# Value products of two attentions taken by head pairs, and low halves of the second attention's outputs made on GpSimd

## Chip, cores and metric

One core of one Trainium2 chip. The metric is the device time of one execution in microseconds (us): before the change 1065.82 us, median of 3 runs (1065.64 to 1067.22). The engines are named as in the profile: PE is TensorE (PEld its weight loads), DVE is VectorE, ACT is ScalarE, POOL is GpSimd, and SP issues most transfers.

## The reference, cut to what matters

Two transformer blocks run one after the other on 256 tokens of width 1024: the first has two layers, the second one (`DEPTH_2 = 1`), so the kernel has layers 0 to 2. Layer 0 has an attention with 8 heads (query and key width 96, value width 64), layer 1 is convolutional, and layer 2 has an attention with 16 heads of width 64. In both attentions the keys are 256 tokens and 256 context tokens:

```python
s = jnp.einsum('bqhd,bhkd->bhqk', qi, kt).astype(jnp.float32) * scale   # first attention
p = jax.nn.softmax(s, axis=-1).astype(vt.dtype)
return jnp.einsum('bhqk,bhkd->bqhd', p, vt)
# second attention: a bias and a mask are added to the scores of the 256 token keys,
# softmax runs over token and context keys together, then p @ v as above
```

After each attention comes an output projection (1024 by 1024), an update of x, a norm and a feed-forward layer. All is fp32.

## The kernel before, in words

**Projections.** Large products are split in high and low halves: weights arrive in a ring of six raw slots (`w_raw`, 512 KB each), ACT casts the high half (`w_hi`, L703), DVE subtracts to get the low half (`w_lo`, L1205), and PE does three products (L1902 to L1904). Activations are held as `h_hi` and `h_lo`. SP issues the loads in the order of a fixed table (`ada_issue_table`, L98): weight w waits for the split of weight w-6, and `at[w]` says how many of the conditioning blocks (`ada`, through four slots of `a_raw`) are issued ahead of weight w. DVE sums one such block per instruction (L1245); a slot is loaded again only when its block has been summed.

**Attention.** The unit is a block n: one head, one tile of 128 queries, 512 keys. Pass j of the loop handles blocks 2j and 2j+1, which are the two heads of a pair at query tile j % 2; so a head pair p takes passes 2p and 2p+1, that is blocks 4p to 4p+3. PE runs, in pass j: the transposes of blocks 2j and 2j+1 (`turn`, L2069, four of 128 by 128 each), the scores of pass j+2 (`scores`, L2060, two products of 512 columns), and the value products of pass j-1 (`weigh`, L2083: eight products with 64 stationary and 128 moving columns, four key tiles by two heads; the two heads write the two halves of the output partitions). After the second `weigh` of a pair four more products (L2091) spread the inverted row sums beside the output in the same bank. Every fp32 product that isn't a transpose leaves two records.

On the other engines pass j has: DVE finds the row maxima of pass j+1 (first attention L1342 and L1344; second attention adds bias and mask in place, L1332, and reduces, L1339); ACT takes the exponentials of pass j (L810) and copies the transposed blocks of pass j-1 from PSUM to `probT` (L822); in the second attention DVE does every fourth of these copies (L1354). For an output, ACT copies it (L829), DVE multiplies it by the inverted sums (L1364), ACT makes its high half (L833) and DVE its low half (`out_lo`, L1368), which the output projection waits for (`o_lo`). In the first attention DVE also sums one conditioning block a pass; in passes 1 to 4 both split one weight.

Score blocks use four banks, transposed blocks two (block n waits until block n-2 is copied out), outputs two. `probT` has two homes of one pass each: a copy of pass j waits for `weigh(j-2)`, by the semaphore `pv_done`, which rises by two each time.

**Around it.** After the first attention ACT issues the load of the second context (`big<-ctx`, 1 MB, L1062), squares its eight tiles when it has landed (L749), and POOL adds these squares and then those of x (`add_squares`, L636); PE takes the sums (L1986) within the last block of the output projection. After the second attention the output projection has eight weights, of which the fourth is split in pass 4 already and the fifth at the projection's start.

Of the kernel before, what the change touches and what calls it, by code (L numbers as in the profile page):

```python
# [9 lines left out]
P = 128  # L10
# [87 lines left out]
def ada_issue_table():  # L98

    at = {RING + n: 17 + n for n in range(4)}  # L100
    at.update({14: 21, 17: 23, 18: 25, 19: 28, 20: 30, 21: 37, 22: 38, 23: 39, 24: 40, 25: 44, 35: 48})
# [100 lines left out]
def program(nc, weights, ada, xt_in, ctx1_in, ctx2_in, params_in, consts_in, rpb_in, out_t):  # L202
# [5 lines left out]
    with ctx:  # L208
# [39 lines left out]
        probT = work[:, PROBS * 512:].rearrange("p (b e k t) -> p b e k t", b=2, e=2, k=4)  # L248
# [318 lines left out]
        def _(sp):  # L567
            def load_w(w, s):

                if w - RING in WHOLE:  # L570
                    sp.wait_ge(w_used, w - RING + 1)
                elif w >= RING:
                    sp.wait_ge(split_done, splits_to(w - RING))
# [45 lines left out]
        def _(pool):  # L619
# [69 lines left out]
            for h in range(BIAS_HOMES, NA_H):  # L689
                mask_bias(h)  # L690
            add_squares(7)

        @block.scalar
        def _(act):
# [118 lines left out]
            def attention(name, heads, at0, o0, query_scale, w_next, begun=0):  # L813

                def turned(n):
                    if name == "na" and n % 4 == 3:
                        return
                    b = wait_tile(act, (name, "tr", n))
                    j, e = n // 2, n % 2
                    if j >= 2:  # L820
                        act.wait_ge(pv_done, at0 + 2 * (j - 1))
                    nc.scalar.copy(probT[:, j % 2, e, :, :], b[:, :].rearrange("p (k q) -> p k q", k=4))\  # L822
# [369 lines left out]
        def _(dve):  # L1192
# [154 lines left out]
            def attention(name, heads, at0, o0, w_next):  # L1347

                def turned(n):
                    b = wait_tile(dve, (name, "tr", n))  # L1350
                    j, e = n // 2, n % 2
                    if j >= 2:
                        dve.wait_ge(pv_done, at0 + 2 * (j - 1))
                    nc.vector.tensor_copy(probT[:, j % 2, e, :, :], b[:, :].rearrange("p (k q) -> p k q", k=4))\  # L1354
# [19 lines left out]
                for j in range(heads):  # L1374
# [11 lines left out]
                    if j >= 4 and j % 2 == 0:  # L1386
# [5 lines left out]
                out_lo(heads // 2 - 2)  # L1392
# [506 lines left out]
        def _(pe):  # L1899
# [163 lines left out]
            def attention(name, heads, at0, rows, values, values_ready, begun):  # L2063
# [574 lines left out]
```

## Time and profile before

| | us |
|---|---|
| median of 3 runs | 1065.82 |
| the profiled execution | 1069.91 |
| its span | 1068.1 |
| PE busy | 1048.2 (98%) |
| DVE busy | 779.7 (73%) |
| ACT busy | 552.6 (52%) |
| POOL busy | 115.7 (11%) |
| chain that ended last | PE 88%, DVE 5%, DMA 3%, issue 2% |

The span is the profiled execution's, which is 4.1 us slower than the median of the timed runs, 1.8 us of this outside the span. PE's ends are modelled, so its busy time is not PE at its peak; what a stage costs is read from the starts of its groups.

### The profile page before, as it was taken

The numbers are of one execution on the slowest core, as the hardware profiler recorded it, in microseconds if no ns is written. First come the engines' busy times: TensorE is split into PE (matmuls) and PEld (weight loads), VectorE is DVE, ScalarE is ACT, GpSimd is POOL, SyncE is SP. The second block draws the span as 40 slices with busy tenths as digits, with TensorE's granted clock in tenths as the row PEclk, the third lists the DMA queues.
The fourth block names the chain that finished last, engine by engine and source line by source line (L and its number), as shares of the span: only waits on it lengthen the run. The fifth ranks groups of instructions, "written<-read, shape, count | busy, mean of one in ns | idle before, by whom it ended". The sixth has DMA issues, their size and how long they took to land.

```text
span 1068.1 us, 20130 instructions
## 1 busy us (share of the span) xinstructions
PE 1048.2 (98%) x7862; PEld 950.1 (89%) x7862; DVE 779.7 (73%) x1381; ACT 552.6 (52%) x951; POOL 115.7 (11%) x133
## 2 busy tenths in 40 slices
PE   6999999999999999999999999999999999999998
PEld 1887787999999989888999999888866799999998
DVE  2697777788887678847677775697439877777876
ACT  4646766444344485555445444546337665454442
POOL 2200012000000037410000000400331020000000
PEclk9999998999999999999999999999999999999999
DMA  9982274989898726465787775387550054656551
GB/s 361 410 315 93 76 246 181 345 344 337 330 354 319 272 64 253 138 255 204 274 288 273 280 269 207 111 291 261 135 99 31 4 187 146 197 166 206 166 189 41
DMA packets 68593, 232.83 MB, mean 218 GB/s; under 512 B 12144, under 2 KB 12432, under 8 KB 68144
## 3 DMA queue, kind: packets, MB, share of 16 engines
q1 hardware_dynamic: 62496, 227.20, 59.6%
q0 software_dynamic: 5888, 3.73, 1.6%
q10 hardware_dynamic: 144, 1.05, 0.3%
q8 instruction: 39, 0.64, 0.2%
q14 instruction: 26, 0.21, 0.1%
HBM read 230.85 MB, written 1.05 MB: 217 GB/s over the span
## 4 chain that ended last, share of the span: by engine, by line
PE 88%; DVE 5%; DMA 3%; issue 2%; ACT 1%; SPq 0%; DVEq 0%; ACTq 0%
PE bank L1902 26%; PE bank L1904 25%; PE bank L1903 25%; PE bank L2427 3%; PE bank L1929 2%; DMA w_raw<-weights 2%; DMA a_raw<-ada 2%; PE bank L2060 2%; DVE bank L1332 1%; PE bank L2069 1%; PE bank L2083 1%; PE bank L1986 1%; DVE w_lo L1205 1%; PE bank L1958 1%; PE bank L2309 1%
## 5 line engine op out<-in xcount | busy, mean ns | idle before, releaser
L1902 PE MATMUL bank<-h_hi,w_hi 128*128 128x256 f32 (+2 forms) x1408 | 404.8, 288 | 3.4 <-DVE h_lo L1853 1.7
L1904 PE MATMUL bank<-h_hi,w_lo 128*128 128x256 f32 (+2 forms) x1408 | 401.7, 285 | 0.0
L1903 PE MATMUL bank<-h_lo,w_hi 128*128 128x256 f32 (+2 forms) x1408 | 401.1, 285 | 0.0
L1205 DVE TENSOR_TENSOR w_lo<-w_raw,w_hi 128x1024 fp32r<-128x1024 f32 x271 | 327.6, 1232 | 64.8 <-ACT w_hi L703 63.4
L703 ACT CAST w_hi<-w_raw 128x1024 fp32r<-128x1024 f32 x271 | 275.5, 1045 | 65.2 <-PE bank L1904 56.8
L1902 PEld LDWEIGHTS bank<-h_hi,w_hi 128*128 128x128 f32 x1408 | 267.5, 190 | 11.4 <-issue 5.2
L1903 PEld LDWEIGHTS bank<-h_lo,w_hi 128*128 128x128 f32 x1408 | 268.0, 190 | 1.3 <-issue 0.2
L1904 PEld LDWEIGHTS bank<-h_hi,w_lo 128*128 128x128 f32 x1408 | 268.0, 190 | 1.0
L1902 PE MATMUL bank<-g_hi,w_hi 128*128 128x256 f32 x528 | 148.9, 282 | 0.0
L1904 PE MATMUL bank<-g_hi,w_lo 128*128 128x256 f32 x528 | 148.8, 282 | 0.0
L1903 PE MATMUL bank<-g_lo,w_hi 128*128 128x256 f32 x528 | 148.7, 282 | 0.0
L636 POOL TENSOR_TENSOR big<-big 128x256 f32<-128x256 f32 x39 | 40.5, 1039 | 595.9 <-ACT big L749 594.2
L1902 PEld LDWEIGHTS bank<-g_hi,w_hi 128*128 128x128 f32 x528 | 99.5, 188 | 0.3 <-issue 0.2
L1245 DVE SCALAR_TENSOR_TENSOR a_raw<-a_raw,bias 128x1024 f32<-128x1024 f32 x80 | 98.8, 1239 | 1.1 <-DMA a_raw<-ada 1.0
L1904 PEld LDWEIGHTS bank<-g_hi,w_lo 128*128 128x128 f32 x528 | 99.5, 189 | 0.0
L1903 PEld LDWEIGHTS bank<-g_lo,w_hi 128*128 128x128 f32 x528 | 99.5, 188 | 0.0
L868 ACT ACTIVATE work<-bank 128x256 f32<-128x256 f32 x44 | 16.9, 384 | 133.3 <-PE bank L1904 133.3
L1902 PE MATMUL bank<-w_hi,h_hi 128*128 128x512 f32 (+1 forms) x180 | 72.1, 400 | 1.7 <-ACT big L1015 1.7
L1903 PE MATMUL bank<-w_lo,h_hi 128*128 128x512 f32 (+1 forms) x180 | 70.8, 393 | 0.0
L1904 PE MATMUL bank<-w_hi,h_lo 128*128 128x512 f32 (+1 forms) x180 | 70.7, 393 | 0.0
L1473 DVE TENSOR_TENSOR work<-work,bank 128x256 f32<-128x256 f32 x44 | 18.5, 421 | 57.4 <-ACT work L868 57.4
L761 ACT ACTIVATE h_hi<-big,mods 128x256 fp32r<-128x256 f32 x56 | 26.6, 505 | 42.1 <-DVE big L1293 41.9
(210 smaller groups left out, 1241.0 us busy)
## 6 DMA issues: line engine op xcount, KB each, us to landing
w_raw<-weights SPq DMA_DIRECT2D x281, 512.0 KB, 4.9
a_raw<-ada SPq DMA_DIRECT2D x140, 512.0 KB, 5.4
vals<-ada SPq DMA_DIRECT2D x4, 512.0 KB, 8.7
a_raw<-rpb POOLq DMA_DIRECT2D x9, 224.0 KB, 14.7
bias<-rpb POOLq DMA_DIRECT2D x7, 224.0 KB, 8.2
xT<-xt SPq DMA_DIRECT2D x1, 1024.0 KB, 9.5
big<-ctx SPq DMA_DIRECT2D x1, 1024.0 KB, 14.3
big<-ctx ACTq DMA_DIRECT2D x1, 1024.0 KB, 8.0
```

Of the source, the lines that this page charges most:

```text
L636: nc.gpsimd.tensor_tensor(v[:, 0, :], v[:, 0, :], v[:, k, :], ADD).then_inc(added, 1)
L703: nc.scalar.copy(w_hi[:, s, :], w_raw[:, s, :]).then_inc(hi_done, 1)
L761: nc.scalar.activation(h_hi[:, k, c0:c0 + T], tmp[:, k, :], ACT.Identity, bias=sh).then_inc(hhi_ready, 1)
L1205: nc.vector.tensor_tensor(w_lo[:, s, :], w_raw[:, s, :], w_hi[:, s, :].bitcast(fp), SUB)\
L1245: nc.vector.scalar_tensor_tensor(out=a_raw[:, s, :], in0=a_raw[:, s, :], scalar=1.0, in1=cond_row[later], op0=MUL, op1=MUL, accum_out=flat ...
L1473: nc.vector.tensor_tensor(gate_f[:, s, :], act_f[:, s, :], bank[b][:, T:2 * T], MUL).then_inc(ff_mul, 1)
L1902: nc.tensor.matmul(out, a_hi, b_hi, start=start, stop=False)
L1903: nc.tensor.matmul(out, a_hi, b_lo, start=False, stop=False)
L1904: return nc.tensor.matmul(out, a_lo, b_hi, start=False, stop=stop)
L1929: ins = nc.tensor.matmul(b[32 * part:32 * part + 2, :], cs[:, g // (MODS // AGRP), k, :], home[:, s, (k % 2) * 512:(k % 2 + 1) * 512], sta ...
L2060: nc.tensor.matmul(b[:, :], q[:, t * P:(t + 1) * P], k, start=True, stop=True)\
L2427: ins = nc.tensor.matmul(b[:, 0:T], w_raw[:, w % RING, k * P:(k + 1) * P], h_whole[k], start=(k == 0), stop=(k == KT - 1))
```

## The change

Value products now run once per head pair: `weigh(p)` follows pass 2p+2 and takes eight products with 256 moving columns (both query tiles, read from `probT` in two stretches of 128) where two calls had eight of 128 each. It waits for all four blocks of the pair. `probT` gets a second home for a whole pair in two raw weight slots, those of weights `W_OUT0 + 4` and `W_OUT2 + 4` and the ones after them. So SP waits at each of these two weights until the attention's last value product is done, and ACT waits, before the first copy into that home, for the splits of the last weights that lay there; and conditioning blocks up to the 40th are issued ahead of weight 19 (`W_OUT0 + 4`) instead of between weights 19 and 24. `pv_done` now rises by two per pair. In the second attention the low halves of outputs 0 to 6 are made on POOL; DVE makes the last one.

```diff
-    at.update({14: 21, 17: 23, 18: 25, 19: 28, 20: 30, 21: 37, 22: 38, 23: 39, 24: 40, 25: 44, 35: 48})
+    at.update({14: 21, 17: 23, 18: 25, 19: 40, 25: 44, 35: 48})
...
-        probT = work[:, PROBS * 512:].rearrange("p (b e k t) -> p b e k t", b=2, e=2, k=4)
+        by_pair = lambda a: a.rearrange("p (t e k q) -> p t e k q", t=2, e=2, k=4)
+        spare = (W_OUT0 + LEAD) % RING
+        probT = [by_pair(work[:, PROBS * 512:]), by_pair(w_raw[:, spare:spare + 2, :].rearrange("p s b -> p (s b)"))]
...
+                if w == W_OUT0 + LEAD:
+                    sp.wait_ge(pv_done, MLA_H)
+                if w == W_OUT2 + LEAD:
+                    sp.wait_ge(pv_done, MLA_H + NA_H)
...
+            for p in range(NA_H // 2 - 1):
+                pool.wait_ge(o_hi, 16 + p + 1)
+                nc.gpsimd.tensor_tensor(h_lo[:, p, 0:T], o_unit[:, p % 2, :], h_hi[:, p, 0:T].bitcast(fp), SUB)\
+                    .then_inc(o_lo, 1)
...
+                    if n == 4:
+                        act.wait_ge(split_done, splits_to(w_next - 1))
                     b = wait_tile(act, (name, "tr", n))
                     j, e = n // 2, n % 2
-                    if j >= 2:
-                        act.wait_ge(pv_done, at0 + 2 * (j - 1))
+                    if j >= 4:
+                        act.wait_ge(pv_done, at0 // 2 + 2 * (j // 2 - 1))
...
+                    if name == "na":
+                        dve.wait_ge(o_lo, o0 + p)
...
-                    if j >= 4 and j % 2 == 0:
+                    if name == "mla" and j >= 4 and j % 2 == 0:
                         out_lo(j // 2 - 2)
...
-                out_lo(heads // 2 - 2)
+                if name == "mla":
+                    out_lo(heads // 2 - 2)
...
-                def weigh(j):
-                    p, t = j // 2, j % 2
-                    if j == 0:
+                def weigh(p):
+                    if p == 0:
                         pe.wait_ge(v_ready, values_ready)
-                    pe.wait_ge(*turned_by(name, at0, 2 * j))
-                    pe.wait_ge(*turned_by(name, at0, 2 * j + 1))
-                    b = write_tile(pe, (name, "o", p)) if t == 0 else bank[tiles[(name, "o", p)][0]]
+                    for n in range(4 * p, 4 * p + 4):
+                        pe.wait_ge(*turned_by(name, at0, n))
+                    b = write_tile(pe, (name, "o", p))
                     for kt in range(4):
                         for e in range(2):
-                            ins = nc.tensor.matmul(b[e * VH:(e + 1) * VH, t * P:(t + 1) * P], values(2 * p + e, kt),
-                                                   probT[:, j % 2, e, kt, :], start=(kt == 0), stop=(kt == 3))
+                            out = b[e * VH:(e + 1) * VH, 0:T].rearrange("p (t q) -> p t q", t=2)
+                            ins = nc.tensor.matmul(out, values(2 * p + e, kt), probT[p % 2][:, :, e, kt, :],
+                                                   start=(kt == 0), stop=(kt == 3))
...
-                    if j:
-                        weigh(j - 1)
-                weigh(heads - 1)
+                    if j and j % 2 == 0:
+                        weigh(j // 2 - 1)
+                weigh(heads // 2 - 1)
```

## Rows read from the trace of the kernel before

**Rows 1.** Windows: stretch, then busy us per engine, PE clock, DMA share, GB/s.

```profile
117.00:145.50 28.50, 28.46 (x251) 19.50 (x249) 25.02 (x56) 25.07 (x55) 0.00 (x0) 1.00 0.57 194
796.00:849.50 53.50, 52.49 (x506) 35.02 (x505) 45.85 (x87) 40.28 (x101) 3.59 (x4) 1.00 0.07 21
```

**Rows 2.** Timeline of PE, second attention: start us, us, engine, line, operation.

```profile
800.85 1.09 PE L2083 MATMUL bank<-work,vals 128*64 128x128 f32 x16
...
835.17 1.09 PE L2083 MATMUL bank<-work,vals 128*64 128x128 f32 x16
836.19 1.09 PE L2069 MATMUL bank<-con,work 128*128 128x128 f32 x8
837.21 1.13 PE L2060 MATMUL bank<-big 64*128 64x512 f32 x4
838.27 1.09 PE L2083 MATMUL bank<-work,vals 128*64 128x128 f32 x16
839.20 0.61 PE L2091 MATMUL bank<-con,rinv 128*64 128x128 f32 x8
839.73 1.09 PE L2069 MATMUL bank<-con,work 128*128 128x128 f32 x8
...
846.50 0.66 PE L2069 MATMUL bank<-con,work 128*128 128x128 f32 x4 [0.52 <-ACT work L822]
847.09 2.04 PE L2083 MATMUL bank<-work,vals 128*64 128x128 f32 x32
```

**Rows 3.** Timeline of PE, first attention.

```profile
118.18 1.88 PE L2060 MATMUL bank<-big 96*128 96x512 f32 x4
119.90 1.04 PE L2069 MATMUL bank<-con,work 128*128 128x128 f32 x8
120.78 1.88 PE L2060 MATMUL bank<-big 96*128 96x512 f32 x4
122.59 1.09 PE L2083 MATMUL bank<-work,vals 128*64 128x128 f32 x16
...
143.06 1.98 PE L2083 MATMUL bank<-work,vals 128*64 128x128 f32 x32
144.86 0.62 PE L2091 MATMUL bank<-con,rinv 128*64 128x128 f32 x8
```

**Rows 4.** Timeline of ACT, first attention: copies out of the transposed banks.

```profile
122.87 0.61 ACT L822 COPY work<-bank 128x512 f32<-128x512 f32 x1
...
138.70 0.59 ACT L822 COPY work<-bank 128x512 f32<-128x512 f32 x1
...
142.73 1.07 ACT L822 COPY work<-bank 128x512 f32<-128x512 f32 x2
```

**Rows 5.** Timeline of ACT, second attention: exponentials of blocks 5 and 13.

```profile
801.33 0.69 ACT L810 ACTIVATE work<-bank,nmax 128x512 f32<-128x512 f32 x1
...
815.19 0.69 ACT L810 ACTIVATE work<-bank,nmax 128x512 f32<-128x512 f32 x1
```

**Rows 6.** Timeline of DVE, second attention.

```profile
818.75 0.42 DVE L1368 TENSOR_TENSOR h_lo<-ada_s,h_hi 128x256 fp32r<-128x256 f32 x1
819.08 0.62 DVE L1332 TENSOR_TENSOR bank<-bank,a_raw 128x256 f32<-128x256 f32 x1
...
847.20 0.69 DVE L1354 COPY work<-bank 128x512 f32<-128x512 f32 x1
```

**Rows 7.** DMA issues from 140 to 175: KB each, median us to landing.

```profile
w_raw<-weights SPq DMA_DIRECT2D x9, 512.0 KB, 5.5
...
big<-ctx ACTq DMA_DIRECT2D x1, 1024.0 KB, 8.0
```

**Rows 8.** Timeline behind the first attention: ACT, POOL and PE's weight loads.

```profile
154.48 2.57 ACT L749 ACTIVATE big<-big 128x256 f32<-128x256 f32 x8 [5.55 <-DMA big<-ctx]
...
155.28 13.26 POOL L636 TENSOR_TENSOR big<-big 128x256 f32<-128x256 f32 x10 [83.18 <-ACT big L749]
...
168.66 1.41 PEld L1986 LDWEIGHTS bank<-con,big 128*128 128x128 f32 x12 [0.16 <-issue]
```

More of the change, by code:

```diff
@@ L246, in program @@
         prob = work[:, 0:PROBS * 512].rearrange("p (b t) -> p b t", b=PROBS)
-        probT = work[:, PROBS * 512:].rearrange("p (b e k t) -> p b e k t", b=2, e=2, k=4)
+        by_pair = lambda a: a.rearrange("p (t e k q) -> p t e k q", t=2, e=2, k=4)
+        spare = (W_OUT0 + LEAD) % RING
+        probT = [by_pair(work[:, PROBS * 512:]), by_pair(w_raw[:, spare:spare + 2, :].rearrange("p s b -> p (s b)"))]
+        assert spare == (W_OUT2 + LEAD) % RING and spare + 1 < RING
         nmax = sb("nmax", [P, 32])
@@ L817, in turned @@
                         return
+                    if n == 4:
+                        act.wait_ge(split_done, splits_to(w_next - 1))
                     b = wait_tile(act, (name, "tr", n))
                     j, e = n // 2, n % 2
-                    if j >= 2:
-                        act.wait_ge(pv_done, at0 + 2 * (j - 1))
-                    nc.scalar.copy(probT[:, j % 2, e, :, :], b[:, :].rearrange("p (k q) -> p k q", k=4))\
+                    if j >= 4:
+                        act.wait_ge(pv_done, at0 // 2 + 2 * (j // 2 - 1))
+                    nc.scalar.copy(probT[j // 2 % 2][:, j % 2, e, :, :], b[:, :].rearrange("p (k q) -> p k q", k=4))\
                         .then_inc(pT_ready, 1)
@@ L1351, in turned @@
                     j, e = n // 2, n % 2
-                    if j >= 2:
-                        dve.wait_ge(pv_done, at0 + 2 * (j - 1))
-                    nc.vector.tensor_copy(probT[:, j % 2, e, :, :], b[:, :].rearrange("p (k q) -> p k q", k=4))\
+                    if j >= 4:
+                        dve.wait_ge(pv_done, at0 // 2 + 2 * (j // 2 - 1))
+                    nc.vector.tensor_copy(probT[j // 2 % 2][:, j % 2, e, :, :], b[:, :].rearrange("p (k q) -> p k q", k=4))\
                         .then_inc(pT_other, 1)
@@ L2085, in weigh @@
                             if kt == 3:
                                 ins.then_inc(pv_done, 1)
-                    if t == 1:
-                        pe.wait_ge(rinv_ready, at0 // 4 + p + 1)
-                        for n in range(4):
-                            e, t = n % 2, n // 2
-                            ins = nc.tensor.matmul(b[e * VH:(e + 1) * VH, T + t * P:T + (t + 1) * P],
-                                                   rinv[:, 4 * p + n:4 * p + n + 1].broadcast_to([P, VH]), ident,
-                                                   start=True, stop=True)
-                        ins.then_inc(full_of((name, "o", p)), 1)
+                    pe.wait_ge(rinv_ready, at0 // 4 + p + 1)
@@ L2096, in attention @@
+                    for n in range(4):
+                        e, t = n % 2, n // 2
+                        ins = nc.tensor.matmul(b[e * VH:(e + 1) * VH, T + t * P:T + (t + 1) * P],
+                                               rinv[:, 4 * p + n:4 * p + n + 1].broadcast_to([P, VH]), ident,
+                                               start=True, stop=True)
+                    ins.then_inc(full_of((name, "o", p)), 1)
                 for j in range(begun, 2):
```

## The prediction

> **What bounds the kernel now.** I read the windows by stage first. In both attentions PE is busy nearly throughout: 28.46 of 28.50 us in the first, 52.49 of 53.50 us in the second [rows 1]. But DVE has 25.02 of 28.50 and 45.85 of 53.50 us of its own there, and ACT is close behind it. So PE sets the end with little to spare, and work taken from PE shortens a stage only until a maximum, an exponential or a copy is what PE waits for. The starts of PE's groups give dense prices. Second attention [rows 2]: a pass's transposes 1.02 us (836.19 to 837.21), scores 1.06 (to 838.27), a value call that a transpose follows 1.02 (835.17 to 836.19), one that the inverse sums follow 0.93 (838.27 to 839.20), the inverse sums 0.53. A head pair therefore takes 2 x (1.02 + 1.06) + 1.02 + 0.93 + 0.53 = 6.64 us. DVE in its turn needs about 6.6 us a pair: 5.73 busy (45.85 / 8) and the gaps between dependent instructions. First attention [rows 3]: scores 1.72 us ahead of a transpose (118.18 to 119.90), 1.81 ahead of a value call (120.78 to 122.59), transposes 0.93; a pair 2 x (0.93 + 1.81) + 1.02 + 0.93 + 0.53 = 7.96 us.
>
> **The value products.** No row has 64 stationary by 256 moving columns. Two calls back to back, 16 products of 128 columns, take 1.80 us (143.06 to 144.86) [rows 3]. The two heads use the two halves of PE's columns and overlap. This shows against full-width products: two score products of 512 columns in 1.72 us are 0.43 us per 256 columns, so eight of 256 one by one would be 3.44 us. Lower bound for the new call: half of it, 1.72. Upper bound: 3.44, if long moving operands don't overlap. The score products of the second attention, which use half the rows, do: two of 512 columns in 1.06 us [rows 2], against 1.72. I take 1.75, near the lower end. A pair's values then fall from 1.95 to 1.75 us; in the first attention the odd pass also has the cheap change from scores to transposes, 0.09 less, three times. On PE's account alone: 12 pairs x 0.20 + 3 x 0.09 = 2.7 us. The two stretches of 128 in the moving operand and the home in a weight slot I put at nothing: they change the addresses, not the columns; no row prices it, and at worst they end at the 3.44 above.
>
> **What PE waits for once the calls are batched.** Before, a value call stood between any two passes and hid the chain from scores over maximum and exponential to the next transposes. Now an odd pass is followed by the next pass at once, and the last pair's call waits for all four of its copies. I walk both stages with the rows' starts and 0.06 us from a copy's end to PE.
>
> First attention. Pass 1 ends at 119.90 + 0.88 + 1.72 = 122.50. Block 5 needs the bank of block 3, whose copy starts at 122.87 and takes 0.60 [rows 4], so its transposes begin at 123.53 and not at 122.97; ACT's order in front of it is unchanged. Scores, call and inverse sums: 123.53 + 0.46 + 1.81 + 1.75 + 0.53 = 128.1, against 122.59 + 1.02 + 0.93 + 1.81 + 0.93 + 0.53 = 127.8 before. The next pair is dense, 7.67 against 7.96, and both are at 135.8. In pass 6 block 13 needs the copy that starts at 138.70: transposes from 139.35, 0.46 late, then the call from 139.9 and the inverse sums until 142.2 (before 142.04). In pass 7 the second half of the transposes starts at 142.65, ACT's two copies (1.07 us) [rows 4] run from 142.9 to 144.0, and the call is at 144.03 where before the first of two calls covered these copies from 143.06. It ends at 145.8 and the stage, after the inverse sums (0.62 at its end [rows 3]), at 146.4; before 144.86 + 0.62 = 145.5. The first attention becomes longer by 0.9 us.
>
> Second attention. Dense, the stage was 16 x 1.02 + 14 x 1.06 + 8 x (1.02 + 0.93 + 0.53) = 51.0 us (the first two passes' scores lie ahead of it), and it took 53.3 (796.2 to 849.5), so PE waited 2.3 us. Dense it now is 49.4, with 1.75 + 0.53 a pair. The waits: up to 800.85 nothing changes, and PE has lost 0.5 us by then (796.2 + 2 x 2.08 = 800.36). There the first call stood [rows 2]; now block 5's transposes come next and need its exponential, started at 801.33 [rows 5] and readable 0.83 later (0.69 and the rest of its accumulator read), so that the scores start at 802.16 + 0.59 = 802.75 and not at 801.87: 0.9. The pass ends at 802.75 + 1.06 + 2.28 = 806.1, passes 3, 4 and 5 are dense (2.08, 4.36, 2.08), and PE stands at pass 6 at 814.6. Block 13's exponential starts at 815.19 before [rows 5], now about 0.2 earlier (DVE has one low half less ahead of it, but gets the scores of pass 5 later), readable at 815.8; its bank is free at 815.9; scores from 816.5 instead of 815.6: 0.9 again. Then a pair is 6.44 us and DVE, without its low half, needs 6.3: some 0.1 a pair, 0.3 in all. At the end the second transposes of the last pass need ACT, which before made them start at 846.50 [rows 2]; DVE's saved 2.0 us (below), less what the late scores cost it, bring them to 845.8, 0.5 behind PE's dense place. Before, the first of the last two calls, from 847.09, then hid DVE's copy at 847.20 [rows 2, 6]. Now copy (0.70 after the transposes' start, 0.69 long) and call follow each other, 1.45 us instead of 0.59: another 0.9. Waits 0.5 + 0.9 + 0.9 + 0.3 + 0.5 + 0.9 = 4.0, stage 53.4 against 53.3. Longer by 0.1 us.
>
> **The low halves on POOL.** DVE loses seven instructions of 0.42 us, each of which puts off the next by 0.33 (818.75 to 819.08) [rows 6]; six lie ahead of the last maximum, 2.0 us, already used above. On POOL one costs about what its additions of the same shape cost, 13.26 / 10 = 1.33 us [rows 8], once in 6.5 us, on an engine with 3.59 us of work in this stage [rows 1]. ACT's copy of output p+2 waits for it, three passes later; the projection asks for tile 6 some 4 us into its work. Price nothing. Below nothing it can't go, since the saving is counted; above, at most the last one could stand on the path, 1.3 us, if the projection came to tile 6 before it.
>
> **The loads held back.** SP now starts weight 19 at the end of the last call, near 145.9, and the next five behind it. One takes 5.5 us [rows 7], and 19 can be split by 154, while PE has four weights before it (96 products at 0.12 us, 11.4 us): it is wanted at 157.8. The fifth weight behind the second attention is wanted 11.4 us after that attention too. Nothing for both. Moving the conditioning blocks costs nothing either: the last of the forty still waits for DVE's sum in pass 6, before the stage's end, and ahead of weight 19 nothing is wanted from SP until then. But the context's 1 MB, issued by ACT at 154.48 - 8.0 = 146.48 [rows 7, 8], will be issued near 147.4 with 3 MB of weights around it. Its squares start POOL's ten additions (155.28 to 168.54), and PE's L1986 starts again at 168.66 [rows 8], right behind the last: this chain is tight, and its whole slack is the 0.9 us by which PE is late. I put the landing 1.1 us later, 0.2 beyond that slack. Bounds 0 and 4: as long as before from its issue, or 5 us later behind all six weights, less 0.9.
> The Trainium skill says (DMA: Bandwidth & Descriptors, Issuing engines are not separate DMA queues) that transfers started by different engines run on the same 16 DMA engines and interleave. By it the context shares the rate with the weights wherever they overlap. How far it is slowed no row shows; by the rule the 0.2 could become any part of the 4, never less than 0.
>
> **Sum.** 0.9 + 0.1 + 0.2 = +1.2 us: span 1069.3, the profiled execution 1071.1. The timed runs lie 4.1 us below it, so the median goes from 1065.8 to 1067.0.
>
> **Rivals.** (1) PE's account is what counts: the waits of my walk are smaller, because ACT and DVE, released earlier, run ahead as they do in the steady passes. Then the 2.7 us are gained, 1063.1. For it: PE's 98% and both stages' busy shares [rows 1]; against it: DVE and ACT are nearly full too, and the last call has nothing to hide its copies. (2) Slower, by the context: if its transfer lies behind the weights, POOL's chain starts after 156.2, which is the point from which it decides (155.28 + 0.9), and PE waits at L1986 for every microsecond beyond; at 4 us this is 1065.8 + 0.9 + 0.1 + 4 = 1070.8. For it: 168.66 is already tight; against it: the context has a queue of its own. (3) The heads' long products don't overlap, so the change doesn't do what it says: 12 x (3.44 - 1.75) = 20 us more, 1087. Against it the score rows of the second attention.
>
> **How the numbers follow.** My forecast 0.48, rival 1 0.24, rival 2 0.24, rival 3 0.04. A measurement tells about 0.2% from no change, 2.1 us, so "same" is 1063.7 to 1068.0. The forecast's own error is some 1.3 us either way (the walk's starts); of its chance 0.42 is same and 0.06 slower. Rival 1 is faster but for 0.02, rival 2 slower but for 0.05 (a wait under 1 us), rival 3 slower. Faster 0.22, same 0.49, slower 0.29. The range takes in rivals 1 and 2: 1063.0 to 1070.6.
>
> **What would show it.** In the profile after: twelve value groups of 16 records, 1.75 us long (3.4 means rival 3); PE waiting for ACT before the second transposes of passes 2 and 6 of both stages, and some 0.8 us ahead of each last call; the first projection starting near 146.4 and the second near 850.7 (849.6 and the 1.1 from before); L1368 five times on DVE instead of twelve, and seven low halves on POOL; the first square addition on POOL near 156.4, the last near 169.7, and no more than 0.4 us between PE's two groups at L1986. The forecast is wrong if a stage comes out over 1 us shorter than in the walk, or if PE waits over 1 us at L1986.

## The result and the profile after

The changed kernel takes 1071.64 us (median of 7 runs, 1070.37 to 1073.39); in the same session the kernel before took 1067.22 (7 runs, 1065.64 to 1068.99). The ratio is 1.0045, 95% interval 1.0032 to 1.0057: slower by 0.45%, where I had forecast no change and 1067.0, and outside my range. The profiled execution of the change has a span of 1071.2 us against 1068.1 (forecast 1069.3), and a time of 1072.96 against 1069.91 (forecast 1071.1). Two executions, one of the kernel before with 1134 us and one of e16 with 2566 us, ran at a far lower granted clock (0.847 and 0.397) and are left out of every mean and interval below.

The stages, by the starts of PE's groups in the two profiled executions:

| stretch | before | after | difference | forecast |
|---|---|---|---|---|
| first attention: its first transposes to the projection's first product | 28.16 | 29.33 | +1.2 | +0.9 |
| from there to the feed-forward block's first product | 33.57 | 35.05 | +1.5 | +0.2 |
| from there to the first products behind the norm ahead of the second attention's inputs (about 685) | 505.93 | 505.89 | 0.0 | 0 |
| from there to the second attention | 111.29 | 112.05 | +0.8 | 0 |
| second attention | 53.29 | 53.64 | +0.35 | +0.1 |
| rest | 218.61 | 218.69 | +0.1 | 0 |

(The start of both executions, up to the first attention, differs by -0.7 us. In the nineteen profiled executions, the experiments' included, the first attention begins anywhere from 116.4 to 118.0 us, so I don't count it as the change's.)

The two attentions as windows (stretch, then busy us of PE, PEld, DVE, ACT and POOL, granted clock, DMA share, GB/s), to be set beside [rows 1]:

```profile
116.50:145.90 29.40, 27.71 (x186) 17.55 (x185) 24.85 (x56) 24.91 (x54) 0.00 (x0) 1.00 0.40 126
798.90:852.50 53.60, 50.95 (x376) 30.61 (x376) 43.91 (x80) 39.78 (x100) 9.34 (x11) 1.00 0.04 11
```

PE has 0.75 and 1.5 us less to do than before, and both stages are longer: PE, which was busy for all but 0.04 and 1.0 us, now waits for 1.7 and 2.65. The timeline of PE in the first attention (start us, us, engine, line, operation, number of records, in brackets the idle time before it and what ended it), to be set beside [rows 3]:

```profile
120.08 1.88 PE L2076 MATMUL bank<-big 96*128 96x512 f32 x4
121.80 0.60 PE L2085 MATMUL bank<-con,work 128*128 128x128 f32 x4
122.84 0.66 PE L2085 MATMUL bank<-con,work 128*128 128x128 f32 x4 [0.44 <-ACT work L835]
...
137.76 0.60 PE L2085 MATMUL bank<-con,work 128*128 128x128 f32 x4
138.64 0.65 PE L2085 MATMUL bank<-con,work 128*128 128x128 f32 x4 [0.28 <-ACT work L835]
139.23 1.95 PE L2099 MATMUL bank<-work,vals 128*64 128x256 f32 x16
141.01 0.61 PE L2106 MATMUL bank<-con,rinv 128*64 128x128 f32 x8
141.54 1.09 PE L2085 MATMUL bank<-con,work 128*128 128x128 f32 x8
143.57 1.95 PE L2099 MATMUL bank<-w_raw,vals 128*64 128x256 f32 x16 [0.93 <-ACT w_raw L835]
145.32 0.63 PE L2106 MATMUL bank<-con,rinv 128*64 128x128 f32 x8
```

The new call is 139.23 to 141.01, 1.78 us; its last one 143.57 to 145.32, 1.75. PE waits in passes 2 and 6 and ahead of the last call, at the three places of the walk. The same in the second attention, beside [rows 2]; PE waits in passes 2 and 6 and in and behind the last one:

```profile
804.05 0.66 PE L2085 MATMUL bank<-con,work 128*128 128x128 f32 x4 [0.46 <-ACT work L835]
804.92 0.63 PE L2085 MATMUL bank<-con,work 128*128 128x128 f32 x4 [0.21 <-ACT work L821]
...
817.85 0.66 PE L2085 MATMUL bank<-con,work 128*128 128x128 f32 x4 [0.36 <-ACT work L835]
818.76 0.65 PE L2085 MATMUL bank<-con,work 128*128 128x128 f32 x4 [0.26 <-DVE work L1367]
...
850.20 1.95 PE L2099 MATMUL bank<-w_raw,vals 128*64 128x256 f32 x16 [0.98 <-DVE w_raw L1367]
851.95 0.64 PE L2106 MATMUL bank<-con,rinv 128*64 128x128 f32 x8
```

Behind the first attention the larger part was lost. ACT's timeline there (ACTq is a DMA that it issues), beside [rows 7, 8]:

```profile
146.92 0.38 ACTq L1075 DMA_DIRECT2D big<-ctx  x1
148.86 1.05 ACT L714 CAST w_hi<-w_raw 128x1024 fp32r<-128x1024 f32 x1 [1.54 <-DMA w_raw<-weights]
150.14 1.05 ACT L714 CAST w_hi<-w_raw 128x1024 fp32r<-128x1024 f32 x1 [0.23 <-DMA w_raw<-weights]
156.97 2.57 ACT L760 ACTIVATE big<-big 128x256 f32<-128x256 f32 x8 [5.78 <-DMA big<-ctx]
159.44 0.40 ACT L760 ACTIVATE big<-xT 128x256 f32<-128x256 f32 x1
159.75 1.03 ACT L714 CAST w_hi<-w_raw 128x1024 fp32r<-128x1024 f32 x1
```

The context lands at 156.97, 2.5 us later than before (10.0 us from its issue instead of 8.0), and in ACT's queue its eight squares stand ahead of the split of weight 21, which begins at 159.75 instead of 157.26 (the kernel before):

```profile
157.26 1.04 ACT L703 CAST w_hi<-w_raw 128x1024 fp32r<-128x1024 f32 x1
```

DVE has to wait for ACT's half of that split, and its next update of x (the tile `xT`, L1429) stands behind its own half, in the order of its queue:

```profile
160.81 1.46 DVE L1218 TENSOR_TENSOR w_lo<-w_raw,w_hi 128x1024 fp32r<-128x1024 f32 x1 [2.26 <-ACT w_hi L714]
162.20 1.75 DVE L1258 SCALAR_TENSOR_TENSOR a_raw<-a_raw,bias 128x1024 f32<-128x1024 f32 x1
...
163.88 0.47 DVE L1429 SCALAR_TENSOR_TENSOR xT<-bank,mods,xT 128x256 f32<-128x256 f32 x1
```

PE needs the bank that this update frees (1.14 us of waiting). Later it waits shortly for a square of x from ACT (0.17 us), and not for POOL's sums of the context:

```profile
164.41 0.38 PE L1918 MATMUL bank<-h_hi,w_hi 128*128 128x256 f32 x1 [1.14 <-DVE xT L1429]
...
171.51 0.61 PE L2002 MATMUL bank<-con,big 128*128 128x1 f32 x4 [0.17 <-ACT big L760]
```

### The profile page after: what moved, and what is told of

It is laid out like the page before. It is cut to its first block, busy times and chain, and to the rows that moved or that the text cites. A ratio compares the mean times of both kernels' runs of the same rounds, so it can differ in the third digit from the quotient of the medians.

```text
span 1071.2 us, 19743 instructions
## 1 busy us (share of the span) xinstructions
PE 1044.3 (97%) x7670; PEld 941.9 (88%) x7670; DVE 777.8 (73%) x1374; ACT 552.2 (52%) x951; POOL 119.3 (11%) x140
## 4 chain that ended last, share of the span: by engine, by line
PE 84%; DVE 8%; DMA 4%; ACT 1%; issue 1%; SPq 0%; DVEq 0%; ACTq 0%
PE bank L1918 24%; PE bank L1920 24%; PE bank L1919 24%; PE bank L2442 3%; DVE w_lo L1218 2%; PE bank L1945 2%; DMA w_raw<-weights 2%; PE bank L2076 2%; DMA a_raw<-ada 2%; PE bank L2099 1%; DVE a_raw L1258 1%; PE bank L2085 1%; DMA big<-ctx 1%; PE bank L1974 1%; PE bank L2002 1%
```

## The experiments

Seventeen kernels, five to twelve executions each, against the kernel before in the same session. Where PE's clock is granted at 1.2 GHz differs from one execution to the next, and that blurs effects of 1 us: the 142 executions of the kernel before in these sessions cover 1064 to 1072 us, on average 1070.3 us at a mean granted clock of 0.990 (14 executions) and 1064.6 at 0.998 (16). So beside the ratio I give the mean time brought to one clock, 0.994, by the slope within all kernels (0.62 us for each 0.001), as the difference to the kernel before (1067.98): "at equal clock". By it the change costs +3.8 us. These differences carry an error of 0.4 to 0.9 us. The last columns are from one profiled execution of each: the stretches of the two attentions; when the context landed, counted from the projection's first product (issue plus time to landing); how long PE idled between that product and the feed-forward block (gaps of 0.15 us and more), and how long that stretch was; and how much of it ran at 1.2 GHz.

| kernel | ratio, 95% interval | at equal clock | 1st attention | context landed | PE idle behind | stretch behind | of it at 1.2 GHz | 2nd attention |
|---|---|---|---|---|---|---|---|---|
| before | 1 | 0 | 28.16 | +9.1 | 0.0 | 33.57 | 6.8 | 53.29 |
| after | 1.0045 (1.0032, 1.0057) | +3.8 | 29.33 | +11.0 | 1.3 | 35.05 | 6.8 | 53.64 |
| e1 lows on DVE | 1.0042 (1.0029, 1.0055) | +4.8 | 29.43 | +10.7 | 2.0 | 32.76 | 0 | 54.39 |
| e2 hold only | 1.0011 (0.9998, 1.0025) | +1.8 | 28.17 | +8.5 | 1.55 | 35.17 | 6.8 | 53.27 |
| e3 first by tile | 1.0001 (0.9987, 1.0014) | +0.4 | 28.16 | +7.2 | 0.0 | 30.49 | 0 | 53.98 |
| e4 context early | 1.0012 (0.9999, 1.0025) | +1.3 | 29.34 | +3.2 | 0.0 | 33.32 | 6.8 | 53.45 |
| e5 before, context early | 1.0003 (0.9986, 1.0021) | -0.1 | 28.16 | +7.6 | 0.0 | 30.47 | 0 | 53.59 |
| e6 second pairs, context early | 1.0008 (0.9992, 1.0024) | +0.1 | 28.17 | +5.8 | 0.0 | 30.47 | 0 | 53.70 |
| e7 context early, ends halved | 1.0020 (1.0007, 1.0032) | +1.9 | 28.37 | +4.4 | 1.8 | 35.38 | 6.8 | 53.05 |
| e8 two held | 1.0039 (1.0024, 1.0053) | +3.2 | 29.42 | +10.3 | 1.2 | 34.90 | 6.8 | 53.55 |
| e9 homes swapped | 1.0038 (1.0019, 1.0057) | +3.2 | 29.34 | +10.7 | 1.4 | 32.28 | 0 | 53.46 |
| e10 swapped, ends halved | 1.0039 (1.0023, 1.0056) | +2.0 | 28.38 | +9.9 | 0.9 | 36.01 | 10.2 | 52.71 |
| e11 part in every pass | 1.0044 (1.0029, 1.0058) | +3.7 | 29.13 | +10.2 | 1.4 | 32.19 | 0 | 53.34 |
| e12 e11, context early | 1.0015 (1.0001, 1.0028) | +2.3 | 29.12 | +4.9 | 0.3 | 32.28 | 3.4 | 53.33 |
| e13 weights behind context | 1.0050 (1.0031, 1.0069) | +5.8 | 29.33 | +5.9 | 3.8 | 35.79 | 3.4 | 53.71 |
| e14 before, context late | 0.9988 (0.9975, 1.0001) | -0.2 | 28.16 | +8.5 | 0.0 | 33.33 | 6.8 | 53.29 |
| e15 second pairs, last halved | 0.9978 (0.9966, 0.9990) | -0.7 | 28.16 | +7.7 | 0.0 | 33.28 | 6.8 | 52.53 |
| e16 e10, context early | 0.9981 (0.9965, 0.9997) | -0.1 | 28.38 | +7.8 | 0.0 | 33.39 | 6.8 | 53.05 |
| e17 before, context later | 1.0026 (1.0010, 1.0042) | +1.3 | 28.16 | +9.9 | 0.9 | 31.55 | 0 | 53.28 |

**One part at a time (e1 to e4).** e1 puts the seven low halves back on DVE:

```diff
-                    if name == "na":
-                        dve.wait_ge(o_lo, o0 + p)
-                    if name == "mla" and j >= 4 and j % 2 == 0:
+                    if j >= 4 and j % 2 == 0:
                         out_lo(j // 2 - 2)
```

> The changed kernel with the seven low halves of the second attention back on DVE. Theory: they are worth what DVE was spared; with them on DVE the late maxima of this stage come about 0.3 us later each in the even passes, so the stage from the second attention's first transposes to the projection becomes 0.3 to 1.5 us longer than the 53.65 us of the changed kernel, and the time is 1072 to 1073 us (ratio to before 1.005 to 1.006). Rival: the low halves on GpSimd are themselves a cost, because a two-input GpSimd operation slows DVE's operations beside it or the output buffer comes free later; then the stage becomes shorter than 53.65 us, by 0.5 us or more, and the ratio falls below 1.004.

The second attention grows to 54.39 us, 0.75 more, and the time by 1.0 at equal clock (five executions; the error is 0.8, and the ratio, 1.0042, doesn't show it). The low halves on POOL are a gain of some 0.75 us. Of the seven on POOL in the changed kernel six took 0.63 to 0.72 us and one 1.72, 0.83 on average.

e2 is the kernel before with the two waits of SP and the new table, e3 the change without its first attention:

> The kernel before with only the held-back loads: the fifth weight behind each attention and those after it wait for the last value product, and the conditioning table is moved as in the change; value products, homes and low halves are untouched. Theory: the held loads put the context's landing later than 8.0 us from its issue and ACT's queue then holds the split of weight 21, so the stretch from the first projection's start to the first product of the feed-forward block grows by 1.3 to 1.8 us (33.5 to about 35), and the whole by as much: 1068.5 to 1069 us by the median of before, ratio 1.0012 to 1.0017. Rival: late loads cost nothing by themselves, and that stretch grew for another reason (the attention's end has another shape); then the stretch stays at 33.5 us and the ratio at 1.000.

> The changed kernel with its first attention as before (value products by 128 columns, one home, no load held back there, the conditioning table of before); the second attention stays by pairs with its low halves on GpSimd. Theory: this takes away 1.1 us of the first attention and 1.5 of the stretch behind it, so 4.8 becomes about 2 us and the ratio 1.0015 to 1.0025; the stage of the second attention stays at 53.6 us. Rival: most of the loss lies in or ahead of the second attention and only looked otherwise in one profiled execution; then the ratio stays at 1.003 or more.

e3 takes 3.4 of the 3.8 us away: nearly all of the loss hangs on the first attention. e2 costs 1.8 us at equal clock with value products as before, but not by the way I had written. Its context landed early (7.5 us from its issue), and its second held weight late. ACT's timeline, and PE's:

```profile
149.21 1.05 ACT L707 CAST w_hi<-w_raw 128x1024 fp32r<-128x1024 f32 x1 [2.11 <-DMA w_raw<-weights]
153.88 1.05 ACT L707 CAST w_hi<-w_raw 128x1024 fp32r<-128x1024 f32 x1 [3.62 <-DMA w_raw<-weights]
154.83 2.56 ACT L753 ACTIVATE big<-big 128x256 f32<-128x256 f32 x8
```

```profile
158.91 0.39 PE L1906 MATMUL bank<-h_hi,w_hi 128*128 128x256 f32 x1 [1.55 <-DVE xT L1417]
```

So weight 20, not weight 19, sets what can be late: DVE splits both before its first update of x, and PE asks for the bank that this update frees as soon as its first four weights are through. Context and held weights land together within some 10 us, now the one first and now the other, and either is late for something.

e4 moves one line of ACT, the context's issue, from behind the last output to behind the last copy:

```diff
                 for n in (2 * heads - 2, 2 * heads - 1):
                     turned(n)
+                if name == "mla":
+                    act.dma_start(ctxT, ctx2_in).then_inc(s_ctx, 16)
```

> The changed kernel with the context's DMA issued by ACT right behind its last copy of transposed probabilities (near 143.3) instead of behind the output of the last pair (146.9). It is then ahead of the six held weights. Theory: it lands near 151.5, ACT's squares start then, the splits of weights 21 and 22 are not held up and the stretch from the first projection to the feed-forward block falls from 35.05 back to 33.5 us or below (to 32.5 if GpSimd's chain was its end); ratio 1.002 to 1.0035. Rival: the stretch is set by the late weights 21 and 22 themselves, not by the context ahead of them on ACT; then PE still waits about 1 us before the third projection of the group and the ratio stays within 0.0005 of 1.0045.

The stretch is 33.32 us, as before with the same 6.8 us at 1.2 GHz in it, PE waits nowhere in it, and 2.5 us are won at equal clock. What remains, 1.3, is about what the first attention is longer by (1.2).

**Is it the context in general, or its company (e5, e6, e8, e9)?**

> The kernel before, in which alone the context's DMA is issued earlier: by ACT behind its last copy of transposed probabilities (near 143.9) instead of behind the last output (146.5). Theory: the context was tight in the kernel before too, so the stretch from the first projection to the feed-forward block loses 0.5 to 2 us and the ratio is 0.998 to 0.9995. Rival: its late landing costs only behind held weights; with the weights early PE is busy throughout that stretch, the stretch stays (33.57 with the clock at half for 6.8 us, about 30.5 to 31 without), and the ratio is 1.000 within 0.001.

> First attention by 128 columns as before, second by pairs with GpSimd's low halves, context's DMA early. Theory: second attention neither gains nor loses (stage 53.3 to 54.0 us), so this comes out as the kernel before with the early context does, ratio within 0.001 of it. Rival: the pairs of the second attention cost what its stage showed in the last run, 0.5 us and more, ratio 0.0005 to 0.001 above it.

The rival of e5 holds: with no weight held, PE doesn't wait where the context lands at +9.1 or sooner, and sooner still gives nothing. e6 is like it within 0.2 us. In e5 the context took 9.8 us from its issue, though no weight was held: two weights and three conditioning blocks were on their way during part of it.

e8 loads the four weights behind the held two ahead of them; e9 swaps the homes, so that the even pairs use the weight slots:

```diff
-                    sp.wait_ge(pv_done, MLA_H)
+                    sp.wait_ge(pv_done, MLA_H - 2)
-                    if n == 4:
+                    if n == 0:
                         act.wait_ge(split_done, splits_to(w_next - 1))
```

> The changed kernel, context's DMA where the change has it, but in the first attention only the two weights whose slots the second home takes are held back: the four behind them are loaded ahead of them during the attention, as before. Theory: with 1 MB instead of 3 MB of weights beside it the context lands 6 to 8.5 us after its issue instead of 10, weight 21 is split in time, PE's wait of 1.1 us goes and the ratio falls from 1.0045 to 1.002 to 1.003; the first attention's stage stays at 29.3 us. Rival: the two weights that are still held are what matters, landing beside the context as late as before; the wait stays, and the ratio too.

> The changed kernel with the two homes of the turned probabilities swapped: the even pairs use the weight slots, the odd ones the old home. The last pair then doesn't need the slots, and the held weights start after the last but one call (near 138.5) instead of after the last (145.5). Theory: what the held loads cost was their coming together with the context; 7 us earlier they have landed before it, PE's wait of 1.1 us and the late context go, the stretch from the first projection to the feed-forward block is that of before (33.6 with the clock at half in it, 30.5 without), and of 4.2 us on the mean of all runs about 1.3 remain, nearly all of it the first attention's 1.1: ratio 1.001 to 1.002. Rival: the late end of the first attention alone pushes the context into the conditioning blocks' loads; then the context takes 9 us or more from its issue here too, and the ratio stays above 1.003.

Both theories fall. In e8 the context still took 9.3 us, and PE waited 0.34 and 0.89. The two held weights beside it were in by 150.7; a conditioning block issued half a microsecond before it took 9.7 us as well. So the number of weights alone doesn't say how long the transfer takes. In e9 I had overlooked what the moved table does to earlier loads: it wants all forty conditioning blocks issued ahead of weight 19, and the last of them waits for DVE's sum in pass 6, which ended at 141.45. SP's timeline in e9 shows that the weights came at 141.93, not at 138.5:

```profile
126.74 15.08 SPq L599 DMA_DIRECT2D a_raw<-ada  x5
141.93 3.07 SPq L581 DMA_DIRECT2D w_raw<-weights  x6
```

Six weights from 142 on are still company for a context issued at 147.06: it took 9.7 us, and PE waited 0.55 us for the update of x and 0.89 for the other consumer of the context's squares, POOL's sums:

```profile
163.95 0.38 PE L1918 MATMUL bank<-h_hi,w_hi 128*128 128x256 f32 x1 [0.55 <-DVE xT L1429]
170.88 1.36 PE L2002 MATMUL bank<-con,big 128*128 128x1 f32 x11 [0.89 <-POOL big L643]
```

**The waits inside the attentions (e7, e10, e11, e12).** e7 and e10 cut the last pair's call in two by queries, the first half ahead of the last copies:

```diff
+                    if j and (j - 1) // 2 in halved:
+                        weigh_half((j - 1) // 2, (j - 1) % 2)
-                weigh(heads // 2 - 1)
+                weigh_half(heads // 2 - 1, 1)
```

> The changed kernel with the early context and, in both attentions, the value products of the last pair in two halves of 128 columns: the first half behind the last pass's transposes, the second at the end. Theory: the first half covers the copies of the last pass, on which PE waited 0.93 us in the first attention and 0.98 in the second; against that stands 0.1 us for two calls instead of one. The first attention's stage falls from 29.3 to 28.5, the second's from 53.6 to 52.8, the time by about 1.6 us from the 1.0012 of the early context, to a ratio of 0.9995. Rival: the copies themselves are late by as much as the half takes, so PE waits for them as long before the second half; then the stages stay at 29.3 and 53.6.

> The same, and the value products of each attention's last pair in two halves of 128 columns. Theory: the two stages fall to 28.4 and 53.05 us as they did before in the run with halved ends, and with the loads early nothing is given back: mean within 0.3 us of the kernel before, ratio 0.9995 to 1.0008, 1 to 1.5 us below the kernel with swapped homes alone. Rival: what the first attention gives is eaten by the context again (its issue follows the last output); then the ratio equals that of the swapped homes.

The stages fall as expected, to 28.4 and to 53.05 and 52.71 us: the uncovered copies were 1.0 us in the first attention and, against the mean of 53.64 by pairs, 0.6 and 0.9 us in the second. But e7, with the context ahead of the weights, got weights 19 and 20 late (ACT split them from 152.76 on, PE waited 1.8 us), and is no faster than e4. e10, with the context behind them, got the context late (0.9 us); at equal clock it is 1.2 us below e9 (error 1.0), but its ratio is the same.

e11 also cuts the calls of all pairs but the last in two by keys, with 256 moving columns in both parts, and takes each output a pass later:

```diff
+                    for kt in (2 * part, 2 * part + 1):
+                    if j >= 2:
+                        weigh(j // 2 - 1, 0) if j % 2 == 0 else weigh((j - 3) // 2, 1)
```

> The same, and the call of every other pair is cut by keys instead of by queries: the products of the first 256 keys stand in the even pass, those of the others in the odd pass behind it, each with 256 moving columns; outputs are copied and scaled a pass later. Every pass from the third on then has a call between its scores and the next transposes, as in the kernel before, and the calls still cost 1.75 us a pair. Theory: the calls' other use, to cover the chain from scores to the next transposes, was what the batching lost; the waits in passes 2 and 6 that lie behind the third pass go (0.28 in the first attention, 0.7 to 1.0 in the second): stages 28.1 and 52.2 us, ratio 0.998 to 0.9995. Rival: DVE and ACT set the pace in the second attention (6.3 to 6.5 us a pair of theirs), so its waits only move to other passes and the stage stays at 53.

> The same as the last, with the context's DMA issued right behind ACT's last copy of transposed probabilities. Theory: with the loads early the context isn't on the path any more, as in the kernel before, where issuing it early gave nothing; ratio within 0.0007 of the last kernel's. Rival: the context is still tight by its squares and GpSimd's chain; then this kernel is 0.5 to 1.5 us faster than the last.

The theory of e11 falls; its stages are 29.13 and 53.34 us, not 28.1 and 52.2. A pair's two parts in it:

```profile
125.69 1.08 PE L2119 MATMUL bank<-w_raw,vals 128*64 128x256 f32 x8
126.71 1.09 PE L2087 MATMUL bank<-con,work 128*128 128x128 f32 x8
...
129.45 1.08 PE L2119 MATMUL bank<-w_raw,vals 128*64 128x256 f32 x8
130.36 0.61 PE L2131 MATMUL bank<-con,rinv 128*64 128x128 f32 x8
```

1.02 + 0.91 = 1.93 us, against 1.02 + 0.93 = 1.95 for the two calls by 128 columns [rows 2]. The 256 columns themselves give next to nothing; what the change won is that PE turns to the values once in a pair and not twice. e12 confirms its rival: 1.4 us less than e11 at equal clock from the early context.

**Company or lateness (e13, e14, e17).** e13 starts the held weights once the context is there:

```diff
                 if w == W_OUT0 + LEAD:
                     sp.wait_ge(pv_done, MLA_H)
+                    sp.wait_ge(s_ctx, 32)
```

> The changed kernel with the six held weights started only once the context has landed; the context's issue is where the change has it (146.9). Theory (shared transfer): alone the context lands 4 to 6 us after its issue, at 151 to 153, its squares and GpSimd's chain no longer end anything; the weights then come from 152 on, the first is still in time for 157.8 and the others arrive faster than PE takes them (1.5 against 2.9 us each). The time falls by 1.5 to 2.5 us against the changed kernel, ratio 1.002 to 1.003. Rival: the context takes 8 us or more even alone (its landing is its own, or the conditioning blocks'), and the weights, now behind it, make PE wait; then the ratio is above 1.005.

Half of the theory is shown: alone (SP's queue is in order, so the conditioning blocks behind the weights were held too), the context took 4.8 us instead of 10.0. The other half, that the weights had time, is refuted; they were split from 154.89 and 156.16 on, and PE waited longest of all:

```profile
154.89 1.05 ACT L715 CAST w_hi<-w_raw 128x1024 fp32r<-128x1024 f32 x1 [7.74 <-DMA w_raw<-weights]
156.16 1.05 ACT L715 CAST w_hi<-w_raw 128x1024 fp32r<-128x1024 f32 x1 [0.21 <-DMA w_raw<-weights]
157.11 2.56 ACT L761 ACTIVATE big<-big 128x256 f32<-128x256 f32 x8
```

```profile
161.18 0.58 PE L1919 MATMUL bank<-h_hi,w_hi 128*128 128x256 f32 x1 [3.79 <-DVE xT L1430]
```

e14 and e17 delay the context in the kernel before, with nothing held:

> The kernel before with the context's DMA issued behind ACT's first two splits of the projection (near 148.9) instead of ahead of them (146.5); no weight is held. Theory: the landing alone decides, from about 154 on, where the slot of the first projection weight comes free and ACT should split the seventh: at 156.5 to 157 the time grows by 1.5 to 2.5 us, ratio 1.0015 to 1.0025. Rival: it takes late weights as well; then the ratio stays within 0.0007 of 1. If the context lands before 155 all the same, the run tells nothing.

> The kernel before with the context's DMA issued by ACT only once DVE has split the second weight behind the attention (near 150.5 instead of 146.5); no weight is held. It should land at 155.5 to 158. Theory: its landing alone decides from about 154 on, since ACT's squares of it stand ahead of the split of the seventh projection weight and of GpSimd's additions: at 157 PE waits 1 to 1.5 us for the xT updates or at the sums, and at equal clock the time grows by 1 to 2.5 us, ratio 1.001 to 1.0025. Rival: without late weights the landing costs nothing up to 158; then the ratio stays within 0.0007 of 1 and PE waits nowhere over 0.2 us in that stretch.

e14 tells nothing on that: the DMA stands behind two splits in ACT's program, but it was issued at 146.75, before they had begun (146.90 to 148.89). e17 makes the issue wait for DVE's split (`act.wait_ge(split_done, splits_to(W_OUT0 + 5))`), and the context, issued at 151.09 and landed 5.0 us later, costs 1.3 us at equal clock (error 0.9; ratio 1.0026, clear of 1); PE waits for POOL's sums:

```profile
156.06 2.57 ACT L749 ACTIVATE big<-big 128x256 f32<-128x256 f32 x8 [6.55 <-DMA big<-ctx]
158.85 1.03 ACT L703 CAST w_hi<-w_raw 128x1024 fp32r<-128x1024 f32 x1
```

```profile
170.28 1.47 PE L1987 MATMUL bank<-con,big 128*128 128x1 f32 x12 [0.92 <-POOL big L636]
```

**What beats before (e15, e16).**

> First attention as before; the second by pairs but for the last pair, whose call is cut in two halves; GpSimd's low halves. Theory: the second stage is 52.7 to 53.1 us against 53.3 of before; 0.2 to 0.6 us faster than before, ratio 0.9992 to 1.0000 by the median. Rival: the stage stays at 53.5 or above as in the run without the halves, and nothing is gained.

> The whole change with homes swapped, last calls halved and the context's DMA early. Theory: stages 28.4 and 52.7 us (28.2 and 53.3 before), the stretch behind the first attention as before; within 0.5 us of before, ratio 0.999 to 1.001. Rival: with the context ahead of them the held weights come late (one of 20 at 153.9 in two other kernels made PE wait 1.6 to 1.8 us); then the ratio is 1.0015 or more.

e15 keeps the first attention as it was, takes the second by pairs, halves its last call and leaves the low halves on POOL: 1066.60 us median, ratio 0.9978, and its second attention is 52.53 us against 53.29. Both the time and the stage are below what I expected. At equal clock it is 0.7 us faster, with an error of 0.5; e14, which changes next to nothing, stood at 0.9988 in the same session, so part of the 0.22% is the session's. e16, the whole change with the three repairs, had 1065.53 us as the median of its other eleven executions (ratio 0.9981), but these had a higher mean clock (0.9962 against 0.9945), and at equal clock it equals before. That the first attention gains nothing by pairs fits both, and its stage (28.38 against 28.16). The end of e15's second attention, with no wait before the values:

```profile
842.21 0.66 PE L2087 MATMUL bank<-con,work 128*128 128x128 f32 x4
843.19 0.66 PE L2087 MATMUL bank<-con,work 128*128 128x128 f32 x4 [0.33 <-ACT w_raw L835]
843.78 2.04 PE L2124 MATMUL bank<-w_raw,vals 128*64 128x128 f32 x32
845.62 0.64 PE L2112 MATMUL bank<-con,rinv 128*64 128x128 f32 x8
```

## Why the prediction was wrong

**Right: the price of the call.** 1.75 forecast, 1.75 to 1.78 measured in all twelve. Rival 3 is refuted. The gain doesn't come from the 256 columns: e11 shows that it is the second turn to the values that was saved.

**Right: the walk through the first attention.** 0.9 forecast, 1.2 measured, with waits of 0.44, 0.28 and 0.93 us at the three places named. The last pair's uncovered copies, the largest of them, are confirmed by e7 and e10 (28.4 us without them). Rival 1, PE's account alone, is refuted by both stages.

**Nearly right: the second attention.** +0.1 forecast, +0.3 measured (mean of seven profiled executions by pairs 53.64, of five as before 53.34). Passes 2 and 6 and the end cost about what the walk said; the pairs after pass 6 ran without a wait where I had put 0.3 us. The low halves on POOL gave 0.75 us (e1), which the walk had inside its 2.0 us of DVE time; one took 0.83 us on average where I had put 1.33.

**Wrong: "The loads held back. ... Nothing for both", and the 0.2 us for the context.** This is the step that failed. Two things in it were off. First, the size of the context's delay: it took 10.0 us from its issue, 2.0 more than before, so it landed 2.5 us later and not 1.1. My bounds, 0 and 4, held that; I stood near the lower end, though the only row on its speed [rows 7] was from a stretch in which only the last weight was still on its way, until 147.9. Issued at this place, the context took 6.2 to 8.0 us in the kernels that hold no weight (before, e3, e14, e15) and 7.5 to 10.0 in those that do (seven of them); e13 shows the mechanism: 4.8 us alone, 10.0 in company. How long it takes in a given company is not worked out (9.8 in e5 with nothing held). Second, the place where it hurts. I looked at POOL's additions only, and took them to be tight from a landing at +9.1 on. That was right (e8 to e11 and e17: PE waits 0.9 us for POOL where the context lands at +9.9 to +10.7; it never does up to +9.1), but ACT's queue is a second way: the squares stand ahead of the split of weight 21, and DVE's updates behind that. In the changed kernel that one cost 1.14 us, and POOL none. And the held weights are not free either: I asked when PE multiplies weight 19, and not who else waits behind the split of weight 20 (e2, e7, e13: 1.6 to 3.8 us).

Moving the conditioning blocks was priced at nothing, and in the changed kernel, where weight 19 starts at 145.55 anyway, nothing contradicts that; in e9 it held the weights until 141.9, whatever the homes.

**Wrong too: "The timed runs lie 4.1 us below it".** That was the distance of one profiled execution of the kernel before, at a mean clock of 0.990, from the median of three timed ones. With the change the distance was 1.3 us, and the median of before itself rose from 1065.82 (3 executions) to 1067.22 (7). Of the 4.6 us by which my median missed, 1.9 lie in the span and 2.8 in this step.

Rival 2, a late context, had the cause, with the point from which it decides (a landing 9 us behind the projection's first product) nearly where I had put it; I gave it 0.24. But its path, PE waiting at the sums (L1986, now L2002) for every microsecond, is not what the changed kernel shows: PE waited 0.17 us there, for ACT, and 1.14 at the bank before. The terms as measured: 1.2 + 0.35 + 1.5 in the profiled execution, and at equal clock 3.8, of which e4 returns 2.5 and e3 3.4.

**Not of the change:** +0.8 us between 685 and the second attention. PE waited 0.93 us for DVE there in the changed kernel, but 0.99 in e14 and 0.60 in e2 too, whose code of that part is that of before, and not in e4 or e9.

**Open:** e4 returns 2.5 us at equal clock, while PE's waits in the profiled execution sum to 1.3. The difference is of the size of the errors, and other executions may have waited longer (2.0 in e1). Whether a wait in that stretch also makes the clock fall more often isn't settled: the profiled executions with waits had from 0 to 10.2 us at 1.2 GHz, those without 0 or 6.8.

## What to carry to other kernels

A call that stands between two dependent steps is also their cover. Batching calls takes the cover from the steps between them, and at the end of a stage the last one stands bare behind its copies. In the second attention here the best was to batch all calls but the last pair's (52.5 to 53.05 us against 53.3); in the first, batching gave nothing.

When a load is held back, ask of each consumer in each in-order queue, not of the multiplication alone, and ask which other transfer it now meets. Here a 1 MB transfer that nobody had touched was the largest loss, and moving its issue by one line (4.2 us earlier) gave 2.5 us back.

## What the runs showed of the hardware

- 64 stationary by 256 moving columns, two heads on the two halves of the columns: 8 products (16 records) in 1.75 to 1.78 us, 4 in 0.91 where the inverse sums follow and 1.02 where transposes do. By 128 columns, 16 products back to back took 1.80 and 1.84 us (1.75 in e11), and two calls of 8 apart 1.95. So the second turn to the values is worth some 0.15 us a pair, more than the wider operand.
- A 1 MB transfer took 4.8 us alone (e13) and 5.0 with one 512 KB block started behind it (e17). In the other kernels that hold no weight it took 6.2 to 9.8 us (e3 6.2, before 8.0, e5 9.8), in those that hold some 6.4 to 10.0 (e4 6.4, the changed kernel 10.0).
- A DMA that stands behind two activations in ACT's program was issued 0.15 us before the first of them began (e14).
- At one and the same place a stretch of 30.5 us (2.4 GHz throughout) took 33.3 us with 6.8 us of it at 1.2 GHz. e3 and e15, whose code is the same there, had the one and the other.
